# Queries and keys of the attention branch computed channel by token, with the rotary step on whole channel rows

## The reference

```python
q_a = partial_rope(a_q.reshape(Bsz, S, A_HEADS, A_HEAD_DIM), pos)
k_a = partial_rope(a_k.reshape(Bsz, S, A_HEADS, A_HEAD_DIM), pos)

def partial_rope(x, pos):        # rd = 16 of 64 channels are rotated, half = 8
    ...
    x1, x2, rest = x32[..., :half], x32[..., half:rd], x32[..., rd:]
    out = jnp.concatenate([x1 * cos - x2 * sin, x1 * sin + x2 * cos, rest], axis=-1)
```

## Time and profile before

| | |
|---|---|
| median of the runs | 505.14 us |
| the profiled execution's own time | 505.35 us |
| its span | 503.6 us |
| TensorE busy | 494.5 us (98%) |
| VectorE busy | 261.4 us (52%) |
| ScalarE busy | 239.2 us (47%) |
| GpSimd busy | 213.0 us (42%) |
| granted TensorE clock over the span | 0.998 of full speed |

### The profile page before, as it was taken

How to read it: one execution, slowest core, us unless ns; L and a number is a source line. 1 busy time by engine, 2 the same in 40 slices (tenths; PEclk the granted TensorE clock), 3 DMA queues, 4 the chain that set the end, 5 groups by cost and what they waited for, 6 DMA issues and landing times.

```text
span 503.6 us, 6823 instructions
## 1 busy us (share of the span) xinstructions
PE 494.5 (98%) x2518; PEld 411.6 (82%) x2518; DVE 261.4 (52%) x575; ACT 239.2 (47%) x434; POOL 213.0 (42%) x130
## 2 busy tenths in 40 slices
PE   8999999999999999999999999999999999999995
PEld 7688888888888888888788888888888888887885
DVE  3865777877899936525655567531111011125433
ACT  6757655555554455536568652413330333152322
POOL 0675131333344444247487451246534663373000
PEclk9999999999999999999999999999999999999999
DMA  8654432212343243112223112043234426453111
GB/s 284 188 153 128 126 87 79 84 48 80 83 111 99 85 117 104 52 43 85 57 70 85 43 43 65 20 125 104 62 87 125 126 58 193 126 149 144 42 55 72
DMA packets 44841, 48.94 MB, mean 97 GB/s; under 512 B 4996, under 2 KB 30212, under 8 KB 44808
## 3 DMA queue, kind: packets, MB, share of 16 engines
q1 hardware_dynamic: 43944, 47.65, 32.3%
q10 hardware_dynamic: 864, 0.86, 0.5%
HBM read 46.40 MB, written 2.11 MB: 96 GB/s over the span
## 4 chain that ended last, share of the span: by engine, by line
PE 94%; DMA 2%; SPq 1%; POOL 1%; ACT 1%; DVE 1%; issue 1%; DVEq 0%
PE pj L1486 24%; PE pj L1487 24%; PE pj L1488 24%; DMA w_raw<-in_w_in 2%; PE ob L1617 2%; PE tr L1606 2%; PE qb L1554 2%; PE qb L1553 2%; PE ob L1487 1%; PE qb L1487 1%; PE ob L1488 1%; PE qb L1488 1%; PE ob L1486 1%; PE qb L1486 1%; PE tr L1541 1%; PE qb L1601 1%
## 5 line engine op out<-in xcount | busy, mean ns | idle before, releaser
L529 POOL TENSOR_TENSOR w_lo<-w_raw,w_hi 128x1024 fp32r<-128x1024 f32 x70 | 168.9, 2424 | 156.3 <-ACT w_hi L875 156.0
L1486 PE MATMUL pj<-w_hi,h_hi 128*128 128x512 f32 x272 | 109.6, 403 | 0.0
L1488 PE MATMUL pj<-w_hi,h_lo 128*128 128x512 f32 x272 | 106.5, 392 | 0.0
L1487 PE MATMUL pj<-w_lo,h_hi 128*128 128x512 f32 x272 | 106.4, 391 | 0.0
L1486 PE MATMUL pj<-h_hi,w_hi 128*128 128x512 f32 (+1 forms) x200 | 78.1, 390 | 1.0 <-DVE h_lo L1129 1.0
L875 ACT ACTIVATE w_hi<-w_raw 128x1024 fp32r<-128x1024 f32 (+1 forms) x72 | 73.5, 1045 | 9.8 <-DMA w_raw<-in_w_out 6.3
L1488 PE MATMUL pj<-h_hi,w_lo 128*128 128x512 f32 (+1 forms) x200 | 77.9, 389 | 0.0
L1487 PE MATMUL pj<-h_lo,w_hi 128*128 128x512 f32 (+1 forms) x200 | 77.8, 389 | 0.0
L1488 PEld LDWEIGHTS pj<-w_hi,h_lo 128*128 128x128 f32 x272 | 51.1, 188 | 11.4
L1486 PEld LDWEIGHTS pj<-w_hi,h_hi 128*128 128x128 f32 x272 | 51.2, 188 | 8.3 <-issue 0.2
L1487 PEld LDWEIGHTS pj<-w_lo,h_hi 128*128 128x128 f32 x272 | 51.3, 188 | 8.0
(11 more groups left out here) (216 smaller groups left out, 817.3 us busy)
## 6 DMA issues: line engine op xcount, KB each, us to landing
w_raw<-in_w_in SPq DMA_DIRECT2D x60, 512.0 KB, 3.6
w_raw<-in_w_out SPq DMA_DIRECT2D x5, 512.0 KB, 3.5
x_tok<-in_x SPq DMA_DIRECT2D x4, 512.0 KB, 5.3
w_raw<-in_w_branch_a SPq DMA_DIRECT2D x8, 256.0 KB, 2.9
w_raw<-in_w_branch_b SPq DMA_DIRECT2D x8, 256.0 KB, 3.3
x_again<-in_x SPq DMA_DIRECT2D x1, 2048.0 KB, 9.3
w_late<-in_w_out SPq DMA_DIRECT2D x3, 512.0 KB, 6.1
out<-y_norm SPq DMA_DIRECT2D x4, 320.0 KB, 2.3
```

Source lines behind the costliest of these rows:

```text
L529: eng.tensor_tensor(lo[:, 0:m], raw_slot(n)[:, 0:m], hi[:, 0:m].bitcast(F32), ALU.subtract).then_inc(lo_by_dve if n in DVE_SLOTS else lo_b ...
L1486: pe.matmul(bank, a_hi, b_hi, start=first, stop=False)
L1487: pe.matmul(bank, a_hi, b_lo, start=False, stop=False)
L1488: return pe.matmul(bank, a_lo, b_hi, start=False, stop=last)
```

## The change

`aq` and `ak` now come out of TensorE channel by token, as `bq` and `bk` did, and the rotary step is done on whole channel rows of 512 tokens:

- ScalarE copies the bank to `q_raw` or `k_raw` (four units of 128 channels each). VectorE multiplies the bank by `cos_t`, a 128 x 512 tile that is 1 in rows that are not rotated, into `q_a` or `k_chan`; that frees the bank.
- Four transfers of 8 partitions by 2048 elements (64 KB each), issued by ScalarE (job `swap`), bring the two halves of the rotated rows, swapped, from the raw tile to `swapped`, whose other rows are 0. Queries' transfers are issued in the quarters of the first `ak` unit, keys' in the last three quarters of `bq` and the first of `bk`.
- GpSimd (job `turn`, eight of them, one every seven quarters from the third quarter of the second `ak` unit) multiplies `swapped` by `sin_t` and adds it.
- For keys, job `parts` three quarters behind each turn: two ScalarE roundings and two VectorE subtractions, now from SBUF (`k_chan`), not from PSUM. They stand in the second and fourth unit of `bk` and in `bv`.
- The eight `stage_chan` jobs of `aq` and `ak` and their rotations are gone. `cos_t` and `sin_t` come out of the `gate_rows` job, which is now one job of four 128-wide transposes whose bank also gives four 16 x 512 ScalarE copies; `gate_cols` is four transposes of 64 rows. GpSimd clears five tiles at its start.

```diff
-STAGED = [u for u in UNITS if u[0] in ("iq0", "iq1", "aq", "ak")]
+STAGED = [u for u in UNITS if u[0] in ("iq0", "iq1")]
+TURNS = [(g, b) for g in TURNED for b in range(KW)]
...
+    for k in range(4):
+        put(first["ak"] + k, "swap", k)
+        put(first["ak"] + 8 + 3 * 7 + k, "swap", KW + k)
+    for m in range(len(TURNS)):
+        p = first["ak"] + 6 + 7 * m
+        put(p, "turn", m)
+        if TURNS[m][0] == "ak":
+            put(p + 3, "parts", m - KW)
...
+            elif UNITS[u] in TURNS:
+                eng.wait_ge(cos_made, TURNS.index(UNITS[u]) + 1)
... (GpSimd)
+            pool.memset(gate_l[:, :, :], 0.0)
+            pool.memset(two_rows[:, :], 0.0)
+            pool.memset(cos_t[:, :], 1.0)
+            pool.memset(sin_t[:, :], 0.0)
+            pool.memset(swapped[:, :, :], 0.0).then_inc(blank_made, 1)
...
+                    if job[0] == "turn":
+                        m = job[1]
+                        g, b = TURNS[m]
+                        pool.wait_ge(rope_made, 4)
+                        pool.wait_ge(swap_in, 64 * (TURNED.index(g) + 1))
+                        pool.tensor_tensor(swapped[:, b, :], swapped[:, b, :], sin_t[:, :], ALU.mult).then_inc(sin_made, 1)
+                        pool.wait_ge(sin_made, m + 1)
+                        pool.wait_ge(cos_made, m + 1)
+                        part = swapped[:, b, :].rearrange("p (t n) -> p t n", n=P)
+                        pool.tensor_tensor(turned_rows(g, b), turned_rows(g, b), part, ALU.add).then_inc(turned, 1)
... (ScalarE)
+                elif kind == "gate_rows":
+
+                    act.wait_ge(blank_made, 1)
                     wait_full(act, job)
+                    for first, dst in ((64, cos_t), (96, sin_t)):
+                        for rows in (slice(0, ROT), slice(A_DIM, A_DIM + ROT)):
+                            act.activation(dst[rows, :], bank_of(job)[first:first + ROT, :], ACT.Copy)\
+                                .then_inc(rope_made, 1)
+                elif kind == "swap":
+
+                    n, k = divmod(job[1], 4)
+                    act.wait_ge(unit_out, UNIT[(TURNED[n], KW - 1)] + 1)
+                    if n:
+                        act.wait_ge(turned, KW * n)
+                    e, half = divmod(k, 2)
+                    to, src = A_DIM * e + HALF * half, A_DIM * e + HALF * (1 - half)
+                    act.dma_start(swapped[to:to + HALF, :, :], raw_chan[n][src:src + HALF, :, :]).then_inc(swap_in, 16)
+                elif kind == "parts":
...
+                    act.wait_ge(turned, KW + b + 1)
+                    for e in range(2):
+                        src, hi, _ = k_part(b, e)
+                        act.activation(hi, src, ACT.Copy).then_inc(k_hi_made, 1)
... (VectorE)
+                elif kind == "parts":
+                    b = job[1]
+                    for e in range(2):
+                        src, hi, lo = k_part(b, e)
+                        dve.wait_ge(k_hi_made, 2 * b + e + 1)
+                        dve.tensor_tensor(lo, src, hi.bitcast(F32), ALU.subtract).then_inc(k_lo_made, 1)
...
-                if g in ("iq0", "iq1", "aq", "ak"):
+                if g in TURNED:
+                    if g == "ak" and j == 0:
+                        dve.wait_ge(swap_in, 64)
+                    if (g, j) == ("aq", 0):
+                        dve.wait_ge(rope_made, 4)
+                    dve.wait_ge(unit_out, u + 1)
+                    dve.tensor_tensor(turned_rows(g, j), pj[u % 2][:, :].rearrange("p (t n) -> p t n", n=P),
+                                      cos_t[:, :].rearrange("p (t n) -> p t n", n=P), ALU.mult).then_inc(cos_made, 1)
... (TensorE)
-                    c = job[1] * B_HEADS
                     for j in range(TILES):
-                        ins = pe.transpose(bank[0:B_HEADS, j * P:(j + 1) * P], gate_l[:, j, c:c + B_HEADS], ident[:, :])
+                        ins = pe.transpose(bank[:, j * P:(j + 1) * P], gate_l[:, j, :], ident[:, :])
...
-                        if g in CHAN_GROUPS:
+                        if g in CHAN_GROUPS + TURNED:
                             a, b = w_part(n, c + j * P, c + (j + 1) * P), h_part(k, 0, SEQ)
```

More of the change, by code:

```diff
@@ L39 @@
 ROT = A_DIM // 4
+ROWS = 64
 HALF = ROT // 2
@@ L122, in plan @@
     put(first["iq0"] + 3, "ik_chan")
-    put(first["iq0"] + 8, "gate_rows", 1)
-    put(first["iq0"] + 8, "gate_rows", 0)
+    put(first["iq0"] + 8, "gate_rows")
     put(first["iq1"] + 3, "gate_cols")
@@ L170 @@
            "score": "q", "qk_b": "q", "qk_a": "q", "pv_b": "o", "pv_a": "o", "kt_b": "tr", "state_b": "o"}
-NOT_PE = ("scales_in", "scales", "decay_b")
+NOT_PE = ("scales_in", "scales", "decay_b", "swap", "turn", "parts")
 def fills():
@@ L421, in hybrid_kernel @@
         en_made = sem("en_made")
+        blank_made = sem("blank_made")
+        rope_made = sem("rope_made")
+        swap_in = sem("swap_in")
+        sin_made = sem("sin_made")
+        cos_made = sem("cos_made")
+        turned = sem("turned")
+        k_hi_made = sem("k_hi_made")
+        k_lo_made = sem("k_lo_made")
         rotated = sem("rotated")
@@ L548, in wait_read @@
             elif kind == "gate_rows":
-                eng.wait_ge(rows_read, 2 - job[1])
+                eng.wait_ge(rows_read, 2)
+                eng.wait_ge(rope_made, 4)
             elif kind == "gate_cols":
@@ L552, in wait_read @@
             elif kind == "stage_chan":
[L553 to L556, removed]
+                eng.wait_ge(part_lo_made, 2 * job[1] + 2)
             elif kind == "score":
@@ L622, in part, with k_part, turned_rows @@
             return src, iq_parts[same, e, b0:b0 + 4, cols], iq_parts[other, e, b0:b0 + 4, cols]
-        def part_unit(job):
-            return job[1] if job[1] < N_IQ else job[1] - TILES
+        def k_part(b, e):
+            same, other = slice(e * A_DIM, (e + 1) * A_DIM), slice((1 - e) * A_DIM, (2 - e) * A_DIM)
+            return k_chan[same, b, :], k_parts[same, e, b, :], k_parts[other, e, b, :]
+        def turned_rows(g, b):
+            return (q_a[:, :, b, :] if g == "aq" else k_chan[:, b, :].rearrange("p (t n) -> p t n", n=P))
         def unit_slots(u):
@@ L1526, in side @@
                     pe.wait_ge(gate_logs, 1)
-                    c = job[1] * B_HEADS
                     for j in range(TILES):
-                        ins = pe.transpose(bank[0:B_HEADS, j * P:(j + 1) * P], gate_l[:, j, c:c + B_HEADS], ident[:, :])
+                        ins = pe.transpose(bank[:, j * P:(j + 1) * P], gate_l[:, j, :], ident[:, :])
                 elif kind == "gate_cols":
                     pe.wait_ge(rows_ready, 1)
-                    for a, row in enumerate((a_row, nm_row)):
-                        for j in range(TILES):
-                            c = (a * TILES + j) * B_HEADS
-                            ins = pe.transpose(bank[:, c:c + B_HEADS], row[:, j * P:(j + 1) * P],
-                                               ident[0:B_HEADS, 0:B_HEADS])
+                    for j in range(TILES):
+                        ins = pe.transpose(bank[:, j * ROWS:(j + 1) * ROWS], two_rows[:, j * P:(j + 1) * P],
+                                           ident[0:ROWS, 0:ROWS])
                 elif kind == "stage_chan":
```

76 lines of the change are left out of this document (41 added, 35 removed).

## The result

The changed kernel takes 507.36 us (median of four runs, 507.15 to 508.46), the kernel before 505.14 (505.14 to 505.3). The ratio is 1.0047, its 95% interval 1.003 to 1.0065: slower by 2.2 us, where 503.6 was forecast. The profiled execution took 507.47 us, its span is 505.6 us.

A forecast was written before the change was run, and what follows sets the result against it. TensorE, busy 494.5 of 503.6 us, was taken to bound the kernel. A gain of 4.46 us less 3.0 us of waiting gave -1.5 us, so 503.6 us (own range 502.9 to 504.8, chance 0.46; whole range 501.2 to 506.6).

The forecast's parts named there:

- The gain on TensorE: TensorE's queue: eight `stage_chan` jobs save 3.76 us, gate rows 0.40, gate columns 0.30; sum 4.46 us if TensorE never waits.
- The start: GpSimd's clearing of tiles, up to 9.6 us, is hidden in its 10.81 us wait for the first weights; costs nothing.
- the swaps: Transfers inside the chip for queries and keys: taken to land after 3 us each.
- the hold in `ak`: First `ak` unit: VectorE held some 3.5 us waiting for the queries' transfers; TensorE loses 0, at most 1 us.
- The third rival: Transfers landing after 4 to 5 us delay the first `ak` unit, turn 4 and `parts` 0: 505.1 us, chance 0.16.
- VectorE's queue without collisions: In `bq` and `bk`, added `parts` work delays the last convolution, so TensorE waits 1.3 us at the second `bv` unit.
- The placing of the collisions: `parts` subtractions wait out GpSimd remainders: 1.0 us at `parts` 0, 0.7 at `parts` 1, together 1.7 us.
- The step that failed: The whole sum: TensorE's gain of 4.46 us less 3.0 us of its waiting gives -1.5 us.
- The cover in `bv`: VectorE's idle 8.51 us at the first head covers its further work in `bv`, with 1 us left.
- The slower one: Rival 4: each of four subtractions finds GpSimd in an instruction, 7.7 us of waiting in `bk` and `bv`: 508.3, chance 0.14.
- The first rival: No collisions of the `parts` subtractions with GpSimd: the loss is 1.3 us and the time 502.0, chance 0.16.
- the second: Rival 2: VectorE keeps up altogether in `bq` and `bk`, so TensorE's gain stays whole: 500.7 us, chance 0.08.

The follow-up runs named there:

- the later versions: Changed kernel with `parts` moved later and the last four top-k pairs two quarters later: 502.27 us (places 37, 48, 51, 58), 501.34 us (51, 53, 56, 59).
- the 2.1 us case: Kernel before, with five further MAX8 on VectorE ahead of the convolution of the fourth `bk` unit: 508.58 us, ratio 1.0063.
- the 4.5 us wait: Kernel before, with nine further MAX8 on VectorE ahead of the convolution of the fourth `bk` unit: 512.16 us, ratio 1.0134.

## Why the prediction was wrong

**The gain on TensorE** was 4.02 us where 4.46 was forecast. Both terms gave a little less. The gate rows take 0.36 us for the 0.79 of before, the gate columns 0.39 for 0.59 (TensorE at 33.13 to 33.49 and 44.19 to 44.58 us): 0.63 saved, 0.70 forecast. Behind them TensorE is 0.50 us ahead, at the last transposes of `iq`, before and then after:

```profile
67.08 0.60 PE L1541 MATMUL tr<-ident,stage 128*128 128x128 f32 x4
```

```profile
66.58 0.60 PE L1616 MATMUL tr<-ident,stage 128*128 128x128 f32 x4
```

From there to `bq` 0 the eight jobs gave 3.52 us where 3.76 was forecast. Put back, they cost 3.69 by the evacuation of `bv` 0 (171.14 for 167.45) and 3.75 by the medians.

**The start, the swaps, the hold in `ak`** cost nothing, as forecast: TensorE has no new wait there. VectorE waits for the queries' transfers once:

```profile
101.32 0.69 DVE L1434 TENSOR_TENSOR k_chan<-pj,cos_t 128x512 f32<-128x512 f32 x1 [1.53 <-DMA swapped<-q_raw]
```

The fourth was issued at 98.17 us, so it took some 3.1 us for the 3 that I had taken. The keys' turn at 144.58 starts without a wait, straight behind a remainder. The third rival, late transfers, is false.

**VectorE's queue without collisions** was too short. I had worked out that TensorE loses 1.3 us to it. With one SBUF operand it loses 2.1: 1.66 at `bv` 1 (from 167.02 to 168.91, less 0.23) and 0.4 at the last unit of `bk`, where I had put nothing. Of the 0.8 us that were missing, some 0.25 are the mask step (that much earlier the last convolution came when the step was free), and 0.24 are two steps from a convolution to a `parts` job (147.83 to 150.18 and 158.31 to 160.66 us, 2.35 each where I had added 2.23). The rest is not separated.

**The placing of the collisions** was right in kind and wrong in place. I had 1.0 us at `parts` 0 and 0.7 at `parts` 1; it was 0 and 2.1. That the sum was off by only 0.4 was luck of phase: a start 0.13 us behind that of a GpSimd remainder cost nearly the whole 2.4 us. TensorE's waiting was 4.2 us in all (3.81 and 0.41) for the 3.0 forecast: 2.1 by the collision for 1.7, and 2.1 by the queue for 1.3.

**The step that failed** is the sum itself: "-4.46 + 3.0 = -1.5 us". It priced a wait of TensorE at its length. Behind the wait the granted clock fell to the 1.2 GHz level, and the matmuls that followed took 1.69 us more in the profiled execution and 2.9 us in another of the same program, the run with the turn at quarter 68 (14 steps from 170.82 to 176.86 us, 6.04 us for 3.17):

```profile
170.82 0.80 PE L1564 MATMUL pj<-w_hi,h_hi 128*128 128x512 f32 x1 [3.67 <-DVE conv_acc L1298]
...
176.86 0.40 PE L1566 MATMUL pj<-w_hi,h_lo 128*128 128x512 f32 x1
```

With the 1.69 us of the profiled execution the account closes: -4.02 + 0.41 + 3.81 + 1.69 = +1.89 us, against 2.0 of the spans. Of the 3.4 us between forecast (-1.5) and profile (+1.9), the clock is 1.7, the longer wait 1.2 and the smaller gain 0.4. Without the slow clock the kernel would have been at 505.8 and thus unchanged, not faster.

**The cover in `bv`** was called 1 us. In the changed kernel VectorE had 3.77 us to spare at the first head, since TensorE itself came late. Once the first wait was taken away, it was gone: the second wait of 1.7 to 1.9 us at the first head.

**The rivals.** The slower one forecast 508.3 from four colliding subtractions; the time came near it, but with one subtraction of the four blocked, and the clock in place of the others. So it was right in its sign, and its sum came near by luck. The first rival (no collisions, 502.0) and the second (VectorE keeps up, 500.7) are out; what they describe is what the later versions reach.

**The Trainium skill**, "SBUF — State Buffer", section "Who interferes with whom", names also `tensor_scalar` among VectorE's instructions that can contend with GpSimd. The mask step is one: 1.55 us beside 0.43, and the trace agrees. The prediction had put the section too simply: a VectorE instruction with at most one SBUF input is free of GpSimd only outside the two-port modes, and the section counts `tensor_scalar` among those that can enter them. No run shows in which mode the mask step ran.

## What to carry to other kernels

A wait of TensorE has two prices, its length and the slow clock behind it: in this kernel 1.5 us cost nothing more, 1.85 us cost 1.4 more in five runs of eleven, 2.1 us cost 1.7 more in three of six, and 3.6 us and up cost some 1.4 to 2.9 more in all runs but one (505.42 us, the turn at quarter 64). The length of the wait is read from one trace of each program. When work moves to an engine that frees TensorE's banks, write down its queue between two banks, and place the movable work behind the last bank, but then look who waits next: here the same backlog came out one stage later, and a second small move was needed to keep the gain. Before an edit that moves a job, look whether the order of instructions changes at all.

## What was not expected of the hardware

- After waits of 3.6 to 4.5 us the granted clock stood at 0.5 for about 3 us or more in each profiled run; after 2.1 us in three of six runs, by their times and mean clocks; after the 1.50 us of the run with one SBUF operand its granted clock stayed at 1.0. In the run with late parts and a 1.85 us wait the times fell in two groups, near 503.6 (six runs, mean clock 0.998 and 0.999) and near 505.0 (five, 0.995 and 0.996); the profiled one is of the second group. With 1.72 us, in the run with only `parts` 0 ahead, none of nine had a mean clock below 0.997. No run here tells what decides between waits of 1.7 and 2.1 us.
- The fall need not come at once: in the 2.1 us case the second matmul after the wait still took 0.39 us, and the 0.63 began 0.9 us behind the first; in the run with the transposes put back it began 1.6 us behind it (174.73 and 176.32 us). Behind the 4.5 us wait the clock was already at 0.5 in the last us of the wait.
- A VectorE instruction with one SBUF input and an SBUF output took 1.55 us beside GpSimd's product, 0.53 when a remainder of GpSimd ended 0.24 us behind its start, and 0.43 with GpSimd idle. The MAX8 and the replacements of the top-k beside it kept their time (for 512 elements 0.70 and 0.68 us at 133.57 and 134.38, while a remainder ran from 132.69 to 135.09).
